# Router on transposed residual rows, modulation at the gather's evacuation, output projection tile by tile

## The chip, the core and the metric

The kernel runs on one core of a Trainium2 chip. The metric is the device time of one execution in microseconds. A core has TensorE (PE in the profile), VectorE (DVE), ScalarE (ACT), GpSimd (POOL) and SyncE (SP), each working through its own queue in order; they hand work to each other by semaphores. DMA queues fill SBUF from HBM.

## What is computed

One decoder layer over 512 tokens of width 1024. The change touches the end of sub-layer 1 and the head of sub-layer 2. Cut to that:

```python
x = x + gate1 * (merged @ w_out[l])
h2 = rmsnorm(x, norm2_g[l]) * (1.0 + scale2) + shift2
# grouped_moe(h2, ...): shared router, 16 experts in 4 groups
logits = t @ router_w + router_b
probs = softmax(logits)
g = argmax over groups of the sum of the top-2 probs
vals, local = top_k(probs of group g, 2)      # weights = vals / sum(vals)
hidden = silu(t @ w_gate) * (t @ w_up)        # per chosen expert
y = sum over experts of weight * (hidden @ w_down)
x = x + gate2 * y
```

`shift2`, `scale2` and the gates are rows of 1024 numbers worked out earlier in the kernel from the condition vector and kept in HBM (`mod_d`).

## The kernel before

Tokens stand in 4 tiles of 128 (`NT`), the width in 8 slices of 128 (`KD`). Every large product is done in three passes (`three`, L612 to L614): both factors are split into a high part in the chip's rounded fp32 (fp32r) and a low rest. A weight chunk of 1 MB is loaded by SP, its high part is written by ACT (`high`, L1087, and `high_e`, L1361) and its low part by DVE (`low`, L1445, and `low_e`, L1759). A chunk then costs PE 48 wide (512-column) multiplies if its 4 products go to 4 banks, or 12 if they go to one.

The output projection `w_out` is done in two halves of 512 columns, `wo0` and `wo1`, two chunks each. `seg` runs chunk by chunk and, in each, over the four token tiles, so that tile m of a half is done only in the last quarter part m of its second chunk. DVE then adds each tile to the residual (`residual`, L1725 and L1727).

After `wo1` comes the router stage. For each token tile: ACT squares and sums the row (`mean_square`, L1318) and takes the root (L1320); DVE inverts it, scales the row (`norm2`, L1734) and adds the shift (L1736), giving fp32 rows `h2f`; ACT and DVE split them into `h2_hi` and `h2_lo` (L1328, L1754); PE turns them (`turn_rows`, L929), ACT copies the turned rows (L1334) and PE multiplies with the router weights (`router`, L936). ACT then has three `high_e` of expert 0 in its queue before the four exponentials (L1368). DVE divides by the sums, ranks (L1778 to L1800), does two `low_e`, and PE counts each expert's tokens in 14 multiplies (L953 to L956). From the counts DVE makes each token's place and the selection matrices (`sel`, L1836).

The experts go in pairs. `gather` (L971) multiplies the split rows with `sel`, 64 multiplies of 256 columns for a pair, in four units of 16; each unit is evacuated by ACT (`hg_high`, L1374) and DVE (`hg_low`, L1862) into `hgT_hi` and `hgT_lo`. Units 2 and 3 reuse the banks of 0 and 1 and wait for their evacuation (`hg_sp`). An expert has 4 up chunks (12 multiplies each) and 2 down chunks. In a pair's second stage PE runs: 4 up chunks, gather units 0 and 1 for the next pair, the down chunks of the expert before, units 2 and 3, the turning of `hid` (L1020). The next stage's up chunk 1 waits for all four units (`hg_sp`, `2 * X + 4`). Six raw buffers and four split buffers carry the chunks; a load waits for `low_e` of the chunk six before it. No planner sets an order: each engine's queue is as written.

## Time and profile before

| | us |
|---|---|
| median of 3 runs | 869.4 |
| lowest and highest | 868.77 and 871.4 |
| the profiled execution | 867.77 |
| its span, first to last instruction | 866.0 |
| PE busy in it | 807.1 (93%) |
| DVE busy | 615.7 (71%) |
| ACT busy | 439.6 (51%) |

The span is divided on the page into 40 slices of 21.65 us; in the row of the granted clock a 9 stands for full speed (2.4 GHz) and a 5 for half (1.2 GHz). Times in the rows are from the span's start. A record of PE carries its pipeline's length, so its start-to-start distance is what an instruction costs in a row of equal ones.

### The profile page before, as it was taken

The numbers are of one execution on the slowest core, as the hardware profiler recorded it, in microseconds if no ns is written. First come the engines' busy times: TensorE is split into PE (matmuls) and PEld (weight loads), VectorE is DVE, ScalarE is ACT, GpSimd is POOL, SyncE is SP. The second block draws the span as 40 slices with busy tenths as digits, with TensorE's granted clock in tenths as the row PEclk, the third lists the DMA queues.
The fourth block names the chain that finished last, engine by engine and source line by source line (L and its number), as shares of the span: only waits on it lengthen the run. The fifth ranks groups of instructions, "written<-read, shape, count | busy, mean of one in ns | idle before, by whom it ended". The sixth has DMA issues, their size and how long they took to land.

```text
span 866.0 us, 10677 instructions
## 1 busy us (share of the span) xinstructions
PE 807.1 (93%) x4014; PEld 643.5 (74%) x4014; DVE 615.7 (71%) x786; ACT 439.6 (51%) x519; POOL 73.4 (8%) x67
## 2 busy tenths in 40 slices
PE   3799999999999889999997779999999999999993
PEld 3687687776666556678886777888888888888882
DVE  4676877425998875536655557888888888888882
ACT  6334224465556345563214607575756566665660
POOL 4020000000000000000000000021111111111111
PEclk9799999999999999999999559999999999999997
DMA  8919993111031112051463245899989898989863
GB/s 257 356 33 386 372 363 141 52 47 50 1 98 49 53 49 74 24 213 63 158 249 132 75 152 179 307 313 318 322 313 337 303 337 310 336 305 334 314 230 51
DMA packets 84330, 174.43 MB, mean 201 GB/s; under 512 B 7696, under 2 KB 27256, under 8 KB 82240
## 3 DMA queue, kind: packets, MB, share of 16 engines
q1 hardware_dynamic: 79200, 156.29, 50.7%
q0 software_dynamic: 5088, 17.59, 8.3%
q8 instruction: 25, 0.41, 0.2%
q14 instruction: 17, 0.14, 0.0%
HBM read 163.34 MB, written 10.52 MB: 201 GB/s over the span
## 4 chain that ended last, share of the span: by engine, by line
PE 81%; DVE 8%; ACT 4%; DMA 3%; issue 2%; SPq 1%; POOL 0%; POOLq 0%; DVEq 0%; ACTq 0%
PE ps L612 19%; PE ps L613 18%; PE ps L614 18%; PE ps L971 7%; PE ps L768 4%; DMA raw<-in_w_in 2%; PE ps L750 1%; DVE w_lo L1445 1%; PE ps L852 1%; PE ps L868 1%; PE ps L880 1%; DMA raw<-in_w_ada 1%; DVE accm L1504 1%; PE ps L783 1%; ACT w_hi L1087 1%
## 5 line engine op out<-in xcount | busy, mean ns | idle before, releaser
L1759 DVE TENSOR_TENSOR w_lo<-raw,w_hi 128x2048 fp32r<-128x2048 f32 x96 | 217.1, 2289 | 22.5 <-ACT w_hi L1361 21.9
L1361 ACT ACTIVATE w_hi<-raw 128x2048 fp32r<-128x2048 f32 x96 | 181.8, 1914 | 15.9 <-PE ps L614 15.9
L612 PE MATMUL ps<-act_lo,w_hi 128*128 128x512 f32 x232 | 98.2, 423 | 7.4 <-DVE act_lo L1487 3.2
L612 PE MATMUL ps<-w_lo,hgT_hi 128*128 128x512 f32 x256 | 101.1, 395 | 0.0
L613 PE MATMUL ps<-w_hi,hgT_lo 128*128 128x512 f32 x256 | 99.7, 390 | 0.0
L614 PE MATMUL ps<-w_hi,hgT_hi 128*128 128x512 f32 x256 | 99.7, 389 | 0.0
L1087 ACT ACTIVATE w_hi<-raw 128x2048 fp32r<-128x2048 f32 (+2 forms) x29 | 52.0, 1794 | 79.7 <-DMA raw<-in_w_in 46.1
L614 PE MATMUL ps<-act_hi,w_hi 128*128 128x512 f32 x232 | 91.1, 393 | 0.0
L613 PE MATMUL ps<-act_hi,w_lo 128*128 128x512 f32 x232 | 90.9, 392 | 0.0
L1445 DVE TENSOR_TENSOR w_lo<-raw,w_hi 128x2048 fp32r<-128x2048 f32 (+2 forms) x29 | 62.0, 2145 | 40.2 <-ACT w_hi L1087 40.1
L591 POOL DMA_INDIRECT out<-ys,slot_tok x16 | 49.3, 3082 | 320.0 <-DVE ys L1855 320.0
L612 PEld LDWEIGHTS ps<-act_lo,w_hi 128*128 128x128 f32 x232 | 43.7, 188 | 32.5 <-issue 16.0
L971 PE MATMUL ps<-sel,act_hi 128*128 128x256 f32 x256 | 64.6, 291 | 3.5 <-DVE sel L1836 3.5
L971 PE MATMUL ps<-sel,act_lo 128*128 128x256 f32 x256 | 64.5, 290 | 0.0
L1374 ACT ACTIVATE hgT_hi<-ps 128x512 fp32r<-128x512 f32 x32 | 19.1, 598 | 79.2 <-PE ps L971 79.2
L614 PEld LDWEIGHTS ps<-w_hi,hgT_hi 128*128 128x128 f32 x256 | 48.1, 188 | 10.2
L612 PEld LDWEIGHTS ps<-w_lo,hgT_hi 128*128 128x128 f32 x256 | 48.1, 188 | 9.6
L613 PEld LDWEIGHTS ps<-w_hi,hgT_lo 128*128 128x128 f32 x256 | 48.1, 188 | 9.4
L971 PEld LDWEIGHTS ps<-sel,act_hi 128*128 128x128 f32 x256 | 51.0, 199 | 4.1 <-issue 3.5
L612 PE MATMUL ps<-w_lo,act_hi 128*128 128x512 f32 x128 | 51.8, 405 | 1.3 <-DVE w_lo L1445 1.3
L612 PE MATMUL ps<-w_lo,hidT_hi 128*128 128x512 f32 x128 | 50.0, 390 | 2.9 <-issue 2.9
L971 PEld LDWEIGHTS ps<-sel,act_lo 128*128 128x128 f32 x256 | 51.0, 199 | 0.5
(260 smaller groups left out, 1497.3 us busy)
## 6 DMA issues: line engine op xcount, KB each, us to landing
raw<-in_w_gate SPq DMA_DIRECT2D x32, 1024.0 KB, 8.5
raw<-in_w_up SPq DMA_DIRECT2D x32, 1024.0 KB, 6.4
raw<-in_w_down SPq DMA_DIRECT2D x32, 1024.0 KB, 8.5
raw<-in_w_in SPq DMA_DIRECT2D x16, 1024.0 KB, 6.7
raw<-in_w_ada SPq DMA_DIRECT2D x16, 1024.0 KB, 7.5
raw<-in_w_ada SPq DMA_DIRECT2D x8, 512.0 KB, 7.0
raw_early<-in_w_ada SPq DMA_DIRECT2D x8, 512.0 KB, 6.2
raw<-in_w_out SPq DMA_DIRECT2D x4, 1024.0 KB, 4.9
```

Of the source, the lines that this page charges most:

```text
L591: pool.indirect_dma_start(out[0], bass.IndirectOffsetOnAxis(slot_tok[:, X % 2:X % 2 + 1], 0), ys[X % 2][:, :], None, compute_op=ALU.add).t ...
L612: pe.matmul(o, a[0], b[1], start=start, stop=False)
L613: pe.matmul(o, a[1], b[0], start=False, stop=False)
L614: return pe.matmul(o, a[0], b[0], start=False, stop=stop)
L750: last = pe.matmul(zt[m % 2][:, r, 0:S - P * i], head(kaT, 2 * hp + r, P * i, P * i + P), head(qaT, 2 * hp + r, P * i, S), start=True, sto ...
L768: pe.matmul(zt[m % 2][:, r, P * (j - i):S - P * i], lhs[:, :], sp_tile(hp, j)[:, r, :], start=False, stop=False, skip_group_check=True)
L971: last = pe.matmul(ps[2 + u % 2][:, 2 * P * (kk % 2):2 * P * (kk % 2) + 2 * P], part[:, tt, P * kk:P * kk + P], sel[:, tt, :, :], start=(t ...
L1087: act.activation(cols(w_hi[spl_slot[w]], 0, top, nk), cols(raw[raw_slot[n]], 0, top, nk), ACT.Copy).then_inc(hi_ready, 1)
L1361: act.activation(e_hi[s_][:, :], e_raw[r][:, :], ACT.Copy).then_inc(e_top, 1)
L1374: act.activation(hgT_hi[:, :, 2 * u:2 * u + 2, :].rearrange("p b k s -> p k b s"), ps[2 + u % 2][:, :].rearrange("p (k b s) -> p k b s", k ...
L1445: dve.tensor_tensor(lo, r, hi.bitcast(F32), ALU.subtract).then_inc(chunk_split, 1)
L1759: dve.tensor_tensor(e_lo[s_][:, :], e_raw[r][:, :], e_hi[s_][:, :].bitcast(F32), ALU.subtract).then_inc(e_split, 1)
```

## The change

- **Router.** It no longer takes modulated rows. PE turns the residual rows themselves (`xres`, raw) and multiplies them with `rwm`, the router weights times (1 + scale2) * norm2_g; DVE then scales the 16 logits of a token with the row's reciprocal deviation (`rstd`) and adds `lbias`, the product of the shift with the router weights plus the router's bias (`logit_bias`, 8 multiplies of 16 columns on PE). Softmax's denominators go, since the ranks and the weights' ratio don't need them.
- **Rows for the gather.** `h2_hi` and `h2_lo` are the residual rows times the reciprocal deviation only, straight from `xres` (`rows_high`, `rows_low`). Scale and shift come in at the evacuation of the gather: `hg_high` is now two instructions of 256 columns with a scale and a bias column, followed by two that take the shift off again (`hm`); `hg_low` two of 256 columns.
- **`wo1`** is done tile by tile (`out_cols`: tile m over the first chunk, then over the second), with the turning and the routers between. It has split buffers 2 and 0, where `wo0` and `wo1` had 0 and 1 in turn.
- **Order.** `low_e(0)` stands ahead of the second half's residual, `low_e(1)` and `low_e(2)` behind the first gather's evacuation; their `high_e` behind the exponentials. Squares are taken by half rows. The count is 5 multiplies instead of 14 (the first of 64 columns, then 64, 48, 32 and 16). Expert chunks 4 and 5 are loaded after `wo1`, into the space of the merged activations.
- **Small loads.** The three broadcast rows of 512 KB become three columns of 1024 single elements, issued once the attention has ended; `gate2` waits for the routers.

Cut to its core; functions of before that go are printed above, and their removal isn't repeated:

```diff
-    e_raw = [raw[2], raw[3], at("raw4", [CH], F32, 136), raw[0], raw[1], at("raw5", [CH], F32, 186)]
-    e_hi = [w_hi[2], w_hi[0], w_hi[1], at("w_hi3", [CH], F32R, 112)]
-    e_lo = [w_lo[2], w_lo[0], w_lo[1], at("w_lo3", [CH], F32R, 120)]
+    e_raw = [raw[2], raw[3], raw[0], raw[1], at("raw4", [CH], F32, 80), at("raw5", [CH], F32, 88)]
+    e_hi = [w_hi[1], w_hi[2], w_hi[0], at("w_hi3", [CH], F32R, 112)]
+    e_lo = [w_lo[1], w_lo[2], w_lo[0], at("w_lo3", [CH], F32R, 120)]
...
-        spl_slot = [(w + 2) % SPL if w < W_PROJ else (w - W_PROJ) % 2 for w in range(N_W)]
+        spl_slot = [(w + 2) % SPL if w < W_PROJ else (w - W_PROJ) % 2 if w < N_W - 2 else (2, 0)[w - N_W + 2] for w in range(N_W)]
...
-                        elif z == 2:
-                            sp.wait_ge(seg_ready, seg_done("oa1", 3))
-                        elif z < 5:
-                            sp.wait_ge(chunk_split, N_RAW - 5 + z + 1)
+                        elif z < 4:
+                            sp.wait_ge(chunk_split, N_RAW - 3 + z)
                         else:
-                            sp.wait_ge(r_ps, NT)
+                            sp.wait_ge(seg_ready, seg_done("wo1", 3))
...
-            pool.wait_ge(seg_ready, seg_done("ob1", 3))
-            for dst, src in ((shift2, mod_d[0][:, D:2 * D]), (amp2, mod_d[1][:, 0:D]), (g2row, norm2_g)):
-                pool.dma_start(dst[:, :], src.partition_broadcast(P).rearrange("p a d -> p (a d)")).then_inc(ld_r2, 16)
+            pool.wait_ge(ob_ps, 2 * NT)
+            for dst, src in ((sc2c, mod_d[1][0, 0:D]), (sh2c, mod_d[0][0, D:2 * D]), (g2c, norm2_g[0])):
+                pool.dma_start(dst[:, :], src.rearrange("(k p) -> p k", p=P), allow_slow_non_contiguous=True
+                               ).then_inc(ld_r2, 16)
...
-            pool.wait_ge(h2_sp, NT)
-            pool.wait_ge(h2T_ps, 2 * NT)
+            pool.wait_ge(r_ps, NT)
...
+            def turn_x1(half, tt):
+                n = n_turned[0]
+                n_turned[0] += 1
+                pe.wait_ge(x1_ready, 4 * half + tt + 1)
+                if n >= 3:
+                    pe.wait_ge(x1T_act, n - 2)
+                for k in range(4):
+                    a = 512 * half + P * k
+                    last = pe.transpose(ps[n % 3][:, P * k:P * k + P], xres[:, tt, a:a + P], ident[:, :])
+                last.then_inc(x1T_ps, 1)
...
+            def router(tt, k0=0, k1=KD):
+                o = ps[4][:, 0:N_EXP] if tt == 3 else ps[3][:, N_EXP * tt:N_EXP * tt + N_EXP]
+                if tt < 3:
+                    pe.wait_ge(x1T_act, 5 + tt)
+                    pe.wait_ge(lb_ok, 1)
+                    pe.wait_ge(r_lg, tt) if tt else None
+                elif k0 == 0:
+                    pe.wait_ge(x1T_act, 4)
+                    pe.wait_ge(x1_ready, 5)
+                else:
+                    pe.wait_ge(x1T_dve, 1)
+                for k in range(k0, k1):
+                    lhs = x1T_a[:, tt, k, :] if k < 4 else x1T_b[tt % 2][:, k - 4, :]
+                    last = pe.matmul(o, lhs, rwm[:, k, :], start=(k == 0), stop=(k == KD - 1))
+                if k1 == KD:
+                    last.then_inc(r_ps, 1)
...
+            out_cols(0, 0, 0, 4)
+            turn_x1(0, 0)
+            turn_x1(0, 1)
+            out_cols(0, 1, 0, 4)
+            turn_x1(0, 2)
+            turn_x1(0, 3)
+            logit_bias()
+            out_cols(1, 0, 0, 4)
+            turn_x1(1, 0)
+            out_cols(1, 1, 0, 4)
+            router(0)
+            out_cols(2, 0, 0, 4)
+            turn_x1(1, 1)
+            out_cols(2, 1, 0, 4)
+            router(1)
+            out_cols(3, 0, 0, 4)
+            turn_x1(1, 2)
+            out_cols(3, 1, 0, 2)
+            router(2)
+            out_cols(3, 1, 2, 4)
+            router(3, 0, 4)
+            turn_x1(1, 3)
+            router(3, 4, KD)
...
+            def x1_copy(half, tt):
+                n = 4 * half + tt
+                act.wait_ge(x1T_ps, n + 1)
+                if half and tt >= 2:
+                    act.wait_ge(r_ps, tt - 1)
+                dst = x1T_b[tt % 2][:, :, :] if half else x1T_a[:, tt, :, :]
+                act.activation(dst, ps[n % 3][:, :].rearrange("p (k s) -> p k s", k=4), ACT.Copy).then_inc(x1T_act, 1)
             def rows_high(tt):
+                act.wait_ge(h2_rs, tt + 1)
+                act.activation(h2_hi[:, tt, :], xres[:, tt, :], ACT.Copy, scale=st[:, tt, 5:6]).then_inc(h2_hiR, 1)
...
+                square(0, tt)
+            act.preload_act_table_set("sqrt_and_others")
+            high_e(0, 0, 1)
+            for tt in range(NT):
+                x1_copy(0, tt)
+            for tt in range(NT - 1):
+                square(1, tt)
+                deviation(tt)
+                x1_copy(1, tt)
+                rows_high(tt)
+            square(1, NT - 1)
+            deviation(NT - 1)
+            act.preload_act_table_set("natural_log_exp_and_others")
+            for tt in range(NT):
+                act.wait_ge(r_lg, tt + 1)
+                act.activation(comb[:, tt, :], comb[:, tt, :], ACT.Exp, bias=nmax[:, tt:tt + 1]).then_inc(r_exp, 1)
+            rows_high(NT - 1)
+            high_e(1, 1, 1)
+            high_e(2, 2, 1)
 
             def hg_high(X, u):
                 act.wait_ge(hg_ps, 2 * X + u + 1)
+                for j in range(2):
+                    kk = 2 * u + j
+                    last = act.activation(hgT_hi[:, :, kk, :], ps[2 + u % 2][:, 2 * P * j:2 * P * j + 2 * P].rearrange(
+                        "p (b s) -> p b s", b=2), ACT.Identity, bias=sh2c[:, kk:kk + 1], scale=amp2c[:, kk:kk + 1])
+                last.then_inc(hg_hi, 1)
+                act.wait_ge(hg_hi, 2 * X + u + 1)
+                for j in range(2):
+                    kk = 2 * u + j
+                    last = act.activation(hm[u % 2][:, j, :, :], hgT_hi[:, :, kk, :].bitcast(F32), ACT.Identity,
+                                          bias=nsh2c[:, kk:kk + 1])
+                last.then_inc(hg_hm, 1)
...
+            def prepare():
+                dve.wait_ge(ld_r2, 48)
+                link(dve.scalar_tensor_tensor(out=amp2c[:, :], in0=sc2c[:, :], scalar=1.0, in1=g2c[:, :], op0=ALU.add,
+                                              op1=ALU.mult))
+                dve.tensor_tensor(rwm[:, :, :], rw[:, :, :], amp2c[:, :].unsqueeze(2).broadcast_to([P, KD, N_EXP]), ALU.mult)
+                dve.tensor_scalar(nsh2c[:, :], sh2c[:, :], -1.0, None, ALU.mult)
+                dve.tensor_copy(shb[:, :, :], sh2c[:, :].unsqueeze(2).broadcast_to([P, KD, P])).then_inc(prep_ok, 1)
+            def rstd(tt):
                 dve.wait_ge(h2_sd, tt + 1)
+                dve.reciprocal(st[:, tt, 5:6], st[:, tt, 5:6]).then_inc(h2_rs, 1)
+            def rows_low(tt):
+                dve.wait_ge(h2_hiR, tt + 1)
+                dve.scalar_tensor_tensor(out=h2_lo[:, tt, :], in0=xres[:, tt, :], scalar=st[:, tt, 5:6],
+                                         in1=h2_hi[:, tt, :].bitcast(F32), op0=ALU.mult, op1=ALU.subtract).then_inc(h2_sp, 1)
+            def logit(tt):
+                dve.wait_ge(r_ps, tt + 1)
+                dve.wait_ge(h2_rs, tt + 1)
+                src = ps[4][:, 0:N_EXP] if tt == 3 else ps[3][:, N_EXP * tt:N_EXP * tt + N_EXP]
+                link(dve.scalar_tensor_tensor(out=comb[:, tt, :], in0=src, scalar=st[:, tt, 5:6], in1=lbias[:, :],
+                                              op0=ALU.mult, op1=ALU.add))
+                dve.tensor_reduce(nmax[:, tt:tt + 1], comb[:, tt, :], AX.X, ALU.max, negate=True).then_inc(r_lg, 1)
...
             raw_chunks(2)
+            prepare()
             dve.wait_ge(ld_x2, 16)
             dve.wait_ge(ld_g1, 16)
+            residual(0, 0)
+            raw_chunks(1)
+            for m in range(1, 4):
                 residual(0, m)
+            dve.wait_ge(h2_ss, NT)
+            dve.tensor_scalar(st[:, :, 4:5], st[:, :, 2:3], 1.0 / D, EPS, ALU.mult, ALU.add).then_inc(h2_base, 1)
...
+            dve.wait_ge(lb_ps, 1)
+            dve.tensor_tensor(lbias[:, :], ps[3][:, 64:64 + N_EXP], rb[:, :], ALU.add).then_inc(lb_ok, 1)
+            dve.wait_ge(lb_ok, 1)
             low_e(0, 0)
+            residual(1, 0)
+            rstd(0)
+            residual(1, 1)
+            rows_low(0)
+            logit(0)
+            rstd(1)
+            residual(1, 2)
+            rows_low(1)
+            logit(1)
+            rstd(2)
+            rows_low(2)
+            residual(1, 3)
+            logit(2)
+            dve.wait_ge(x1T_ps, 2 * NT)
+            dve.wait_ge(r_ps, 2)
+            dve.tensor_copy(x1T_b[1][:, :, :], ps[1][:, :].rearrange("p (k s) -> p k s", k=4)).then_inc(x1T_dve, 1)
+            rstd(3)
+            logit(3)
             dve.wait_ge(r_exp, NT)
...
-            for cc in (1, 2):
-                low_e(cc, cc)
+            rows_low(3)
...
-                dve.wait_ge(hg_hi, 2 * X + u + 1)
-                part = lambda t: t[:, :, 2 * u:2 * u + 2, :].rearrange("p b k s -> p k b s")
-                dve.tensor_tensor(part(hgT_lo), ps[2 + u % 2][:, :].rearrange("p (k b s) -> p k b s", k=2, b=2),
-                                  part(hgT_hi).bitcast(F32), ALU.subtract).then_inc(hg_sp, 1)
+                dve.wait_ge(hg_hm, 2 * X + u + 1)
+                for j in range(2):
+                    kk = 2 * u + j
+                    last = dve.scalar_tensor_tensor(
+                        out=hgT_lo[:, :, kk, :], in0=ps[2 + u % 2][:, 2 * P * j:2 * P * j + 2 * P].rearrange(
+                            "p (b s) -> p b s", b=2), scalar=amp2c[:, kk:kk + 1], in1=hm[u % 2][:, j, :, :], op0=ALU.mult,
+                        op1=ALU.subtract)
+                last.then_inc(hg_sp, 1)
...
+                    low_e(1, 1)
+                    low_e(2, 2)
```

PE at the end of the router stage, before: rows of tile 3 are turned, two routers follow, then the 14 multiplies that count (only the first of them stands here).

```order
L929 MATMUL ps<-ident,h2f_120 128x128 x3
L929 MATMUL ps<-ident,h2f_120 128x128 [waits h2T_sb]
L929 MATMUL ps<-ident,h2f_120 128x128 x3
L936 MATMUL ps<-rw,h2T 128x16 [waits h2T_sb]
L936 MATMUL ps<-rw,h2T 128x16 x7
L936 MATMUL ps<-rw,h2T 128x16 [waits h2T_sb]
L936 MATMUL ps<-rw,h2T 128x16 x7
L954 MATMUL ps<-comb,before 128x16 [waits route_sel]
```

After: of the last tile only its second half is left to turn when `wo1` has ended, and the count is five multiplies.

```order
L956 MATMUL ps<-rwm,x1T_a 128x16 [waits x1_ready,x1T_by_act]
L956 MATMUL ps<-rwm,x1T_a 128x16 x3
L933 MATMUL ps<-ident,xres 128x128 [waits x1T_by_act,x1_ready]
L933 MATMUL ps<-ident,xres 128x128 x3
L956 MATMUL ps<-rwm,x1T_b_120 128x16 [waits x1T_by_dve]
L956 MATMUL ps<-rwm,x1T_b_120 128x16 x3
L1001 MATMUL ps<-comb,before 128x64 [waits route_sel]
L1004 MATMUL ps<-comb,ones 128x64
L1004 MATMUL ps<-comb,ones 128x48
L1004 MATMUL ps<-comb,ones 128x32
```

What moved: three of the four routers and seven of the eight turnings stand among the wide multiplies of `wo1`, ahead of this place.

DVE between the two halves of the output projection, before (`w_lo` here is the second chunk of `wo1`, and `etmp` the residual's product with the gate):

```order
L1725 TENSOR_TENSOR etmp_114<-ps,gate_115 128x512 [waits seg_ready]
L1727 TENSOR_TENSOR xres<-xres,etmp_114 128x512 [waits evac_low]
L1445 TENSOR_TENSOR w_lo_59<-raw_50,w_hi_56 128x2048 [waits hi_ready]
L1745 SCALAR_TENSOR_TENSOR amp_122<-amp_122,g2row 128x1024 [waits ld_rows2]
L1725 TENSOR_TENSOR etmp_113<-ps,gate_115 128x512 [waits seg_ready,dve_chain]
L1727 TENSOR_TENSOR xres<-xres,etmp_113 128x512 [waits evac_high]
L1725 TENSOR_TENSOR etmp_114<-ps,gate_115 128x512 [waits seg_ready]
```

After, from the last residual of the first half to the first of the second:

```order
L1789 TENSOR_TENSOR xres<-xres,etmp_115 128x512 [waits evac_low]
L1787 TENSOR_TENSOR etmp_116<-ps,gate_117 128x512 [waits seg_ready]
L1789 TENSOR_TENSOR xres<-xres,etmp_116 128x512 [waits evac_low]
L1826 TENSOR_SCALAR st<-st 128x4 [waits h2_ss]
L1834 TENSOR_TENSOR lbias<-ps,rb 128x16 [waits logit_bias_ps]
L1830 TENSOR_TENSOR w_lo_59<-raw_51,w_hi_56 128x2048 [waits expert_hi,logit_bias]
L1787 TENSOR_TENSOR etmp_115<-ps,gate_117 128x512 [waits seg_ready]
L1789 TENSOR_TENSOR xres<-xres,etmp_115 128x512 [waits evac_high]
```

What moved: `low_e(0)` (L1830, `w_lo` from `raw`) stands behind a wait for PE's `logit_bias` and ahead of the residual that PE's next turning needs.

DVE from the selection matrices to the first expert's fourth chunk, before:

```order
L1836 TENSOR_TENSOR sel<-iota,posm 128x4x128 x2
L1862 TENSOR_TENSOR hgT_lo<-ps,hgT_hi 128x2x2x128 [waits hg_hi] x4
L1824 CAST slot_t<-tid 128x64
L1825 CAST slot_t<-comb 128x64
L1826 TENSOR_TENSOR slot_t<-comb,slot_t 128x64 [waits dve_chain]
L1759 TENSOR_TENSOR w_lo_148<-raw_49,w_hi_147 128x2048 [waits expert_hi,ld_gate2]
```

After, from the evacuation of gather unit 2:

```order
L1946 SCALAR_TENSOR_TENSOR hgT_lo<-ps,amp2c,hm_145 128x2x128 [waits hg_less_shift]
L1946 SCALAR_TENSOR_TENSOR hgT_lo<-ps,amp2c,hm_145 128x2x128
L1946 SCALAR_TENSOR_TENSOR hgT_lo<-ps,amp2c,hm_146 128x2x128 [waits hg_less_shift]
L1946 SCALAR_TENSOR_TENSOR hgT_lo<-ps,amp2c,hm_146 128x2x128
L1830 TENSOR_TENSOR w_lo_60<-raw_52,w_hi_57 128x2048 [waits expert_hi]
L1830 TENSOR_TENSOR w_lo_58<-raw_49,w_hi_55 128x2048 [waits expert_hi]
L1907 CAST slot_t<-tid 128x64
L1908 CAST slot_t<-comb 128x64
L1909 TENSOR_TENSOR slot_t<-comb,slot_t 128x64 [waits dve_chain]
L1830 TENSOR_TENSOR w_lo_155<-raw_50,w_hi_154 128x2048 [waits expert_hi,ld_gate2]
```

What moved: `low_e(1)` and `low_e(2)`, which stood ahead of the count, stand behind the last unit, and a unit is two instructions.

## Rows read from the trace of the kernel before

**Rows 1.** The page: the granted clock in 40 slices
```profile
PEclk9799999999999999999999559999999999999997
```

**Rows 2.** Windows: us, busy time (and instructions) by engine, granted clock, DMA share, GB/s
```profile
490.00:520.00 30.00, 20.19 (x109) 20.01 (x110) 16.23 (x42) 7.36 (x14) 0.00 (x0) 0.57 0.42 144
...
560.00:600.00 40.00, 40.00 (x217) 34.64 (x216) 34.19 (x26) 24.75 (x19) 6.22 (x2) 1.00 0.93 315
```

**Rows 3.** Chain of work, 448 to 532 us: start, us, what
```profile
485.19 1.80 PE ps L929 x8
...
487.51 5.50 ACT w_hi L1361 x3
493.03 1.28 ACT L1368
...
499.69 0.23 DVE comb L1797
...
509.58 10.60 PE ps L971 x64
...
530.86 0.24 PE ps L614
```

**Rows 4.** Timeline of PE, 467 to 512 us: start, us, instruction, idle time before
```profile
469.42 0.39 PE L614 MATMUL ps<-w_hi,act_hi 128*128 128x512 f32 x1
...
481.76 3.43 PE L936 MATMUL ps<-rw,h2T 128*128 128x16 f32 x16
...
499.97 0.61 PE L954 MATMUL ps<-comb,before 128*128 128x16 f32 x2 [6.35 <-DVE comb L1797]
...
509.58 0.55 PE L971 MATMUL ps<-sel,act_hi 128*128 128x256 f32 x1 [3.46 <-DVE sel L1836]
```

**Rows 5.** Timeline of DVE, same stretch: same columns
```profile
461.76 0.69 DVE L1725 TENSOR_TENSOR etmp<-ps,gate 128x512 f32<-128x512 f32 x1 [8.23 <-PE ps L614]
...
496.10 0.42 DVE L1778 TENSOR_TENSOR r_gt<-comb 128x256 f32<-128x256 f32 x1
...
506.16 0.17 DVE L1805 COPY counts<-ps 128x16 f32<-128x16 f32 x1 [1.11 <-PE ps L956]
```

**Rows 6.** Groups by shape on ACT, then DVE: count, busy, mean ns of one, idle before
```profile
L1374 ACT ACTIVATE hgT_hi<-ps 128x512 fp32r<-128x512 f32 x32 | 19.1, 598 | 79.2 <-PE ps L971 79.2
...
L1256 ACT ACTIVATE lrow<-lrow,nmax 128x256 f32<-128x256 f32 x8 | 4.0, 500 | 4.9 <-DVE nmax L1653 4.9
...
L1275 ACT ACTIVATE obT_hi<-ps 128x256 fp32r<-128x256 f32 x8 | 3.0, 370 | 1.3 <-PE ps L880 1.3
...
L1112 ACT ACTIVATE hfull<-ps,mod 128x512 f32<-128x512 f32 x1 | 0.8, 777 | 2.7 <-DVE mod L1481 2.7
...
L1759 DVE TENSOR_TENSOR w_lo<-raw,w_hi 128x2048 fp32r<-128x2048 f32 x96 | 217.1, 2289 | 22.5 <-ACT w_hi L1361 21.9
...
L1862 DVE TENSOR_TENSOR hgT_lo<-ps,hgT_hi 128x512 fp32r<-128x512 f32 x32 | 21.5, 689 | 25.2 <-ACT hgT_hi L1374 25.2
...
L1592 DVE SCALAR_TENSOR_TENSOR score<-relu_tmp,wi,score 128x256 f32<-128x256 f32 x7 | 3.4, 483 | 0.1
```

**Rows 7.** Timelines of ACT, DVE and PE round one hand-over between expert pairs
```profile
599.75 0.60 ACT L1374 ACTIVATE hgT_hi<-ps 128x512 fp32r<-128x512 f32 x1 [1.32 <-PE ps L971]
...
600.39 0.69 DVE L1862 TENSOR_TENSOR hgT_lo<-ps,hgT_hi 128x512 fp32r<-128x512 f32 x1 [1.23 <-ACT hgT_hi L1374]
...
603.11 4.49 DVE L1759 TENSOR_TENSOR w_lo<-raw,w_hi 128x2048 fp32r<-128x2048 f32 x2
...
602.75 0.39 PE L612 MATMUL ps<-w_lo,hgT_hi 128*128 128x512 f32 x1
```

**Rows 8.** Windows across the fall and the rise of the clock, columns as Rows 2
```profile
474.00:475.00 1.00, 0.00 (x0) 0.00 (x0) 0.96 (x3) 0.91 (x1) 0.53 (x1) 0.88 0.00 0
...
515.50:516.00 0.50, 0.50 (x5) 0.50 (x5) 0.00 (x0) 0.00 (x0) 0.00 (x0) 0.79 0.00 0
```

**Rows 9.** The column load into c_col (1024 single elements): issue to landing
```profile
DMA to landing us min/median/max: 2.2/2.2/2.2
```

186 lines of the change are left out of this document (68 added, 118 removed).

## The prediction, made blind

> **What bounds the kernel now.** I read the page's clock row first: it stands at 9 nearly throughout and falls to 5 in one place, slices 26 and 27 [rows 1]. There the windows show PE busy for 20.19 of 30 us at a clock of 0.57, while in the expert loop it is busy 40.00 of 40 us at full clock, with DVE at 34.64, ACT at 24.75 and a DMA share of 0.93 [rows 2]. So the loop is PE's, and what can be won lies where the clock is low. The chain there is a walk between engines: turnings (485.19), then three weight splits on ACT (487.51, 5.50 us) and a table load (1.28) ahead of the exponentials, DVE's ranking until 499.69 plus 0.23, PE's count, and the first gather at 509.58, itself at half clock for most of its 10.60 us; the first expert's up chunks end at 530.86 + 0.24 = 531.1 [rows 3]. The last wide multiply of `wo1` is issued at 469.42 and one costs 0.227, so `wo1` ends at 469.65 [rows 4]. From there to the gather it is 509.58 - 469.65 = 39.9 us. That is the stretch that the change attacks, and it pays for it before and behind.
>
> **Part 1, `wo1` with work between (a cost).** `wo1` is 96 wide multiplies of 0.227, so it began at 469.65 - 21.8 = 447.9. Put between them now: 7 turnings of four transposes, the shift's product and three routers of 8 multiplies. Before, eight transposes took 1.80 us at half clock [rows 3], 0.225 each; 16 router records (two to a multiply) took 3.43, 0.214 each [rows 4]. `wo1` runs at full clock, so I take half of both: 28 x 0.112 = 3.1 and 64 x 0.107 = 6.8, together 9.9 us. If the narrow records did not gain from the clock it would be 6.3 + 13.7 = 20.0; below 9.9 no reason points.
> There is one more wait. `logit_bias` ends at about 456.9 (12 + 12 wide multiplies, four turnings, itself), and DVE waits for it ahead of `low_e(0)`, 2.29 us [rows 6]. Then the residual of tile 0 takes two instructions of 0.69 [rows 5], so it is ready at 457.3 + 2.3 + 1.4 = 461.0. PE has finished tile 1's first chunk at 459.6 and stands before the turning of tile 0: 1.5 us. Behind it tile by tile DVE's residual (1.4) fits beside 2.7 us of wide multiplies, and ACT's copies too, so I see no second wait. `wo1` now ends at 469.65 + 9.9 + 1.5 = 481.1, which is 11.4 later.
>
> **Part 2, from the last wide multiply to the gather (the gain).** Last tile: residual ready 1.7 us on (482.8), four transposes (0.5), DVE's copy of a 512-column bank (0.69 as for the same width in [rows 6]), the last four router multiplies (8 records, 0.9), all with 0.1 a hand-over: 485.2. ACT squares half a row, takes the root and loads the exponential's table (1.28) meanwhile, until 485.3. Two small DVE instructions for the logits (0.4) and the last exponential (0.3) bring 486.3. From there DVE's ranking is as before less the normalisation: from 496.10 [rows 5] to 499.92 [rows 3], 3.8, so 490.1. The three splits of 5.50 us are gone from this path, and so is any wait for a raw chunk. The count is 10 records for 28: before, from 499.97 [rows 4] to 506.16 [rows 5], 6.2; now 10 x 0.214 = 2.1 plus a pipeline of 0.3, 492.5. `rows_low` of tile 3 (1.3) fits beside it. Then the places and `sel`, 509.58 - 506.16 = 3.4, as before: the gather starts at about 495.9. The stretch is 14.8 us for 39.9, a gain of 25.1. Bounds: four or five hand-overs that I put too short add up to 3; a path in which the exponentials of tiles 0 to 2 are done early takes 1 off.
>
> **Part 3, the gather's evacuation and the first expert (a cost).** The rows show no instruction with scale and bias columns and 256 columns. A plain copy of 512 columns takes 0.598; with both columns (L1112) 0.777, so 0.18 more. A plain copy of 256 takes 0.370, one with a bias column 0.500 [rows 6]. So a unit on ACT is 2 x 0.55 + 2 x 0.50 less an overlap of 0.1 at two places, 1.9 us, for 0.60; on DVE two of 0.483 less 0.1, 0.9, for 0.69. Ends: 1.5 (four plain ones) and 2.5 (no overlap and slow hand-overs).
> The Trainium skill states the same surcharge (ScalarE: Activation LUTs, What ACT_TABLE_LOAD costs): about 93 ns for each column operand, and as much overlap between neighbours. By it a unit would be 2 x 0.585 + 2 x 0.49 - 0.28 = 1.9. The rule speaks against this change, and the rows agree with it.
> In the first gather unit 3 waits for unit 1's evacuation, 2.9 us against one unit's 1.92 of multiplies (16 x 0.12) and its own start-up: 1.2 us of wait. Up chunk 1 then waits for unit 3's evacuation and, behind it, `low_e(1)`: 2.9 + 2.3 = 5.2 against 2.7 of chunk 0, 2.5 us. `low_e(2)` and `low_e(3)` keep up with PE. Together 3.7 us. Both splits had been done before the gather; the cover is gone. The loads are no issue: chunks 4 and 5 start at 481 and are wanted at 510 or later.
>
> **Part 4, the loop.** At each of 7 hand-overs the last unit's ACT copy starts at 599.75, DVE ends at 600.39 + 0.69 = 601.08, and PE wants it at 602.75: slack 1.67 [rows 7]. Added are 1.3 on ACT and 0.2 on DVE, 1.5 us. The slack just holds; I allow 0.1 each, 0.8 in all. The delay is handed on in DVE's queue to the weight split for up chunk 3, which PE starts two chunks later, at 602.75 + 2 x 2.72 = 608.2; the first of the two splits from 603.11 on ended half way, at 605.4 [rows 7], so 1.5 fits. In a pair of 42 us DVE and ACT have idle time to catch up [rows 2]. So nothing accumulates. Ends: 0 and 7 x 1.0.
> The three column loads: in another place such a load of 1024 single elements landed in 2.2 us [rows 9], and here they have over 40 us. I cost them at nothing.
> Of them the Trainium skill says (DMA: Bandwidth & Descriptors, Rules for kernel authors) that a non-contiguous last dimension becomes one descriptor per element and should be avoided; by that rule the change would look bad, but the row shows a small price, and three of them would be well hidden.
>
> **The sum.** -25.1 + 11.4 + 3.7 + 0.8 = -9.2 us. Against the profiled execution that is 867.77 - 9.2 = 858.6; that execution lies 1.6 under the median of the three runs, by which it would be 860.2. I take 859.4 between them.
>
> **The clock.** After the last wide multiply the clock held about 5 us, with a few transposes in them, and fell in the window at 474; it rose in the one at 515.5, 6 us into the gather, although PE had run narrow records from 481.76 to past 487 without a gap [rows 3, 4, 8]. So narrow work does not keep it up. I assume the same two marks: it falls in the tail and the gather's first 6 us run at half.
>
> **Rivals.**
> 1. Smaller gain: `wo1` is stretched more. Narrow records at 0.15 instead of 0.107, or a wait of 1 us before each later turning. For it: each turning waits for a residual that DVE makes behind other work in the same queue. Against: 2.7 us of wide multiplies cover 1.4. Price 3 to 6 us: 863 to 866.
> 2. Slower: the hand-over becomes the loop's bound. ACT's eight added instructions and DVE's two-step units exceed the slack of 1.67 by more than they do in my working. It decides from 1.4 us of loss a hand-over: 7 x 1.4 = 9.8 eats the gain of 10.0 that the sum has without its 0.8, and with 1.5 to 2 us each the time is 869 to 873. For it: the DMA share of 0.93 and DVE's 34.64 of 40 leave little room to catch up [rows 2]. Against: ACT has 15 us idle in 40.
> 3. Larger gain: the tail is 2 us shorter, or the clock rises earlier or never falls (the gather then takes 7.7 for 10.6 us). 853 to 856.
> 4. No change: what is put into `wo1` is as long as what it saves, because the low clock reaches into it. Against: in the attention stage PE mixes narrow and wide work and the row of the clock shows 9 [rows 1]. If it happened, 10 us of wide work at half clock would cost 10 more: 868 to 870.
>
> **Chances.** Forecast (855 to 863) 0.60; rival 1 0.14; rival 2 0.07; rival 3 0.13; rival 4 0.06. A measurement of this kernel can tell 0.3%, 2.6 us, from no change. Below 866.8 lie the forecast, rivals 1 and 3: 0.87. Rival 4 is half within, so same 0.05 and slower 0.08. For 8 in 10 I take the forecast, most of rival 3 and most of rival 1: 853 to 866.
>
> **What would show it.** Right: last wide multiply of `wo1` at 481 with a wait of 1.5 us before the fifth turning; gather at 496; its unit 3 waiting 1.2 us; 2.5 us of wait at expert 0's chunk 1; ACT's evacuation instructions at 0.55 and 0.50; a pair of experts still at 42 us. Wrong: waits of PE on `hg_split` in every pair, a clock of 0.5 inside `wo1`, or a gather start later than 500.

## The result, and the profile after

The changed kernel takes 860.9 us (median of 4 runs, 860.69 to 861.29) beside 870.4 us for the kernel before on the same chip (868.77 to 872.84, 4 runs). The ratio is 0.989, with a 95% interval of 0.986 to 0.992: faster by 1.1%. The forecast was 859.4. On a second chip the changed kernel was measured again (run `c1_changed`, below): 0.989 once more, 0.986 to 0.993.

The profiled execution of the changed kernel has a time of 861.29 us and a span of 859.6, against 867.77 and 866.0 before. So the two traces explain 6.4 us of span; the medians are 9.5 apart. I come back to these 3 us at the end of the point by point part.

The clock row of the page has lost its trough; where [rows 1] show two slices at 5, it now reads:

```profile
PEclk9799999999999999999999889999999999999997
```

TensorE's timeline from `wo1` to the first expert's turning, which answers to [rows 4] (start, us, instruction, idle time before it and what ended it). L933 turns a tile of residual rows, L956 is the router, L1001 and L1004 count, L1021 is the gather:

```profile
450.70 1.03 PE L933 MATMUL ps<-ident,xres 128*128 128x128 f32 x8
...
460.99 0.66 PE L933 MATMUL ps<-ident,xres 128*128 128x128 f32 x4 [1.05 <-DVE xres L1789]
464.24 0.96 PE L956 MATMUL ps<-rwm,x1T_a 128*128 128x16 f32 x8
...
481.60 0.96 PE L956 MATMUL ps<-rwm,x1T_a 128*128 128x16 f32 x8
483.27 0.66 PE L933 MATMUL ps<-ident,xres 128*128 128x128 f32 x4 [0.71 <-DVE xres L1789]
484.71 1.07 PE L956 MATMUL ps<-rwm,x1T_b 128*128 128x16 f32 x8 [0.78 <-DVE x1T_b L1852]
490.50 0.69 PE L1001 MATMUL ps<-comb,before 128*128 128x64 f32 x2 [4.72 <-DVE comb L1881]
490.99 1.83 PE L1004 MATMUL ps<-comb,ones 128*128 128x64 f32 x8
496.28 0.55 PE L1021 MATMUL ps<-sel,h_hi 128*128 128x256 f32 x1 [3.46 <-DVE sel L1919]
502.96 0.38 PE L1021 MATMUL ps<-sel,h_hi 128*128 128x256 f32 x1 [1.05 <-DVE hgT_lo L1946]
512.30 0.47 PE L615 MATMUL ps<-w_lo,hgT_hi 128*128 128x512 f32 x1 [2.51 <-DVE w_lo L1830]
523.16 0.66 PE L1070 MATMUL ps<-ident,hid 128*128 128x128 f32 x4 [0.85 <-DVE hid L1969]
```

The router of the last tile starts at 481.60, right behind the last wide multiply, and the gather at 496.28. Before, that stretch went from 469.65 to 509.58 [rows 3, 4].

The clock in the same stretch (windows; the last four columns are POOL's busy time, the granted clock, the DMA share and GB/s):

```profile
486.00:487.00 1.00, 0.00 (x0) 0.00 (x0) 0.59 (x4) 1.00 (x4) 0.54 (x1) 0.59 0.88 258
496.30:499.00 2.70, 2.70 (x13) 2.70 (x14) 0.00 (x0) 0.00 (x0) 0.00 (x0) 0.50 0.03 6
499.00:500.00 1.00, 1.00 (x7) 1.00 (x7) 0.00 (x0) 0.00 (x0) 0.00 (x0) 0.59 0.00 0
...
514.00:516.00 2.00, 2.00 (x6) 1.63 (x5) 1.97 (x5) 0.00 (x0) 0.00 (x0) 0.50 0.96 338
...
840.00:845.00 5.00, 4.81 (x14) 3.84 (x15) 0.09 (x1) 0.00 (x0) 1.54 (x1) 0.66 0.56 79
```

It falls near 486.2, 4.6 us after the last wide multiply, and is back at 499.8, 3.5 us into the gather. (In a window of one microsecond a clock of 0.59 means that it stood at half for four fifths of it.) Then come two more falls that I had not forecast: at half clock (0.50 in 514 to 516) eight multiplies of the first expert run, soon behind chunk 1's wait of 2.51 us, and again eight of the last down chunks behind the last turning. Both waits stand in TensorE's timeline, the second here:

```profile
836.68 0.60 PE L1070 MATMUL ps<-ident,hid 128*128 128x128 f32 x4
840.19 0.47 PE L615 MATMUL ps<-w_lo,hidT_hi 128*128 128x512 f32 x1 [2.91 <-issue]
...
847.13 0.39 PE L617 MATMUL ps<-w_hi,hidT_hi 128*128 128x512 f32 x1
```

The evacuation of the gather on ScalarE and VectorE, unit 0 of the first gather:

```profile
500.04 1.02 ACT L1429 ACTIVATE hgT_hi<-ps,sh2c,amp2c 128x256 fp32r<-128x256 f32 x2 [8.80 <-PE ps L1021]
501.09 0.91 ACT L1435 ACTIVATE hm<-hgT_hi,nsh2c 128x256 f32<-128x256 f32 x2
502.03 0.88 DVE L1946 SCALAR_TENSOR_TENSOR hgT_lo<-ps,amp2c,hm 128x256 fp32r<-128x256 f32 x2 [5.90 <-ACT hm L1435]
```

And the loop, 40 us of it, to be held against the second window of [rows 2]:

```profile
575.00:615.00 40.00, 40.00 (x216) 34.49 (x215) 34.35 (x34) 29.72 (x31) 4.46 (x3) 1.00 0.93 319
```

The waits of the stretch 550 to 830 us hold one on the evacuation (PEld's; us in total, times, longest):

```profile
PEld ps L615 <- DVE hgT_lo L1946: 1.4, 7, 0.2
```

TensorE is still busy for the whole 40 us. ScalarE has gone up from about 25 to 30. The three column loads, issued from 382.9 on, landed 2.9, 2.9 and 3.3 us later and are first used at 434.8, so they cost nothing, as forecast (op, KB, us from issue to landing):

```profile
sc2c<-mod_scratch POOLq DMA_DIRECT2D x1, 4.0 KB, 2.9
sh2c<-mod_scratch POOLq DMA_DIRECT2D x1, 4.0 KB, 2.9
g2c<-in_norm_g POOLq DMA_DIRECT2D x1, 4.0 KB, 3.3
```

**How the experiments are read.** Single runs of one kernel differ by up to 9 us, and in the profiles most of this arises in the first 100 us. The first turning of `wo1` comes at 450.70 in the profile above, at 454.21 in that of the same kernel on the second chip and at 457.57 in a variant that is identical up to there (e1); of these 6.9 us between first and last, 5.7 stand already at the first product of `acc` with `ones` (99.53 and 105.24). So beside each ratio I cut the profile into stretches by TensorE's own marks: T, the first turning (first L933); G, the gather's first multiply; H, the first turning of `hid`; L, the last turning of `hid`; M, the last multiply. Each number is a difference of two starts in the timeline. For the kernel before, G to H is 531.94 - 509.58. T to G is left blank where the turnings stand behind `wo1`, since T is then another place.

| kernel | T to G | G to H | H to L | L to M | median, us | ratio to before (95%) |
|---|---|---|---|---|---|---|
| before | | 22.36 | 312.98 | 8.84 | 870.4 | |
| changed | 45.58 | 26.88 | 313.52 | 10.45 | 860.9 | 0.989 (0.986 to 0.992) |
| changed, second chip (c1) | 45.50 | 26.86 | 313.43 | 10.44 | 860.9 | 0.989 (0.986 to 0.993) |
| e1_low0 | 44.64 | 26.28 | 313.46 | 10.42 | 858.8 | 0.986 (0.984 to 0.989) |
| e2_low12 | 45.57 | 23.61 | 313.49 | 8.84 | 858.1 | 0.985 (0.982 to 0.988) |
| e3_undo | | 26.91 | 313.44 | 10.45 | 869.5 | 0.999 (0.997 to 1.001) |
| e4_fill | 45.01 | 25.35 | 313.41 | 8.82 | 858.0 | 0.985 (0.982 to 0.987) |
| e5_best | 43.21 | 20.20 | 313.55 | 8.84 | 850.8 | 0.979 (0.976 to 0.982) |
| e6_hm2 | 45.51 | 28.04 | 326.17 | 10.46 | 876.2 | 1.008 (1.005 to 1.010) |
| e7_exps | 49.01 | 26.46 | 313.53 | 10.44 | 864.3 | 0.994 (0.992 to 0.996) |
| e8_fill_two | 45.77 | 26.38 | 313.39 | 8.84 | 861.1 | 0.990 (0.986 to 0.993) |
| e9_before_exps | | 21.49 | 312.98 | 10.44 | 869.2 | 0.999 (0.997 to 1.002) |
| e10_no_fill | 43.79 | 22.26 | 313.49 | 10.43 | 856.7 | 0.985 (0.982 to 0.988) |
| e11_no_shift | 45.57 | 23.62 | 312.95 | 11.71 | 859.7 | 0.989 (0.986 to 0.993) |

The two profiles of the changed kernel agree to 0.1 us in every stretch. Between variants the clock's falls and rises come at other times, and G to H can move by a microsecond through that alone. Each stretch is from one profiled execution, so differences below 1 us in it are read with that in mind. The medians of the kernel before, against which the ratios of the three later comparisons stand, are 871.3 (e1 to e4), 870.9 (c1, e5 to e7) and 869.8 us (e8 to e11).

### The profile page after: what moved, and what is told of

Same layout as the page of the kernel before. It is cut to its first block, busy times and chain, and to the rows that moved or that the text cites. A ratio compares the mean times of both kernels' runs of the same rounds, so it can differ in the third digit from the quotient of the medians.

```text
span 859.6 us, 10823 instructions
## 1 busy us (share of the span) xinstructions
PE 801.4 (93%) x4010; PEld 633.8 (74%) x4012; DVE 612.0 (71%) x820; ACT 479.9 (56%) x618; POOL 74.3 (9%) x67
## 4 chain that ended last, share of the span: by engine, by line
PE 82%; DVE 7%; ACT 4%; DMA 3%; issue 2%; SPq 1%; POOL 0%; POOLq 0%; DVEq 0%; ACTq 0%
PE ps L615 20%; PE ps L617 19%; PE ps L616 19%; PE ps L1021 7%; PE ps L771 4%; DMA raw<-in_w_in 1%; PE ps L753 1%; PE ps L855 1%; DVE w_lo L1507 1%; PE ps L871 1%; PE ps L883 1%; DMA raw<-in_w_ada 1%; DVE accm L1566 1%; PE ps L786 1%; ACT w_hi L1137 1%
## 5 line engine op out<-in xcount | busy, mean ns | idle before, releaser
L1830 DVE TENSOR_TENSOR w_lo<-raw,w_hi 128x2048 fp32r<-128x2048 f32 x96 | 215.6, 2286 | 16.8 <-ACT w_hi L1402 16.8
L1402 ACT ACTIVATE w_hi<-raw 128x2048 fp32r<-128x2048 f32 x96 | 180.0, 1909 | 11.3 <-PE ps L617 11.3
L1021 PE MATMUL ps<-sel,h_hi 128*128 128x256 f32 x256 | 63.6, 288 | 4.5 <-DVE sel L1919 3.5
L1021 PE MATMUL ps<-sel,h_lo 128*128 128x256 f32 x256 | 63.4, 287 | 0.0
L617 PEld LDWEIGHTS ps<-w_hi,hgT_hi 128*128 128x128 f32 x256 | 48.4, 189 | 10.4
L1429 ACT ACTIVATE hgT_hi<-ps,sh2c,amp2c 128x256 fp32r<-128x256 f32 x64 | 32.7, 562 | 41.7 <-PE ps L1021 41.7
L1021 PEld LDWEIGHTS ps<-sel,h_hi 128*128 128x128 f32 x256 | 50.1, 196 | 5.3 <-issue 3.5
L617 PEld LDWEIGHTS ps<-act_hi,w_hi 128*128 128x128 f32 x232 | 44.0, 190 | 10.0
```

Of the source, the lines that this page charges most:

```text
L617: return pe.matmul(o, a[0], b[0], start=False, stop=stop)
L1021: last = pe.matmul(ps[2 + u % 2][:, 2 * P * (kk % 2):2 * P * (kk % 2) + 2 * P], part[:, tt, P * kk:P * kk + P], sel[:, tt, :, :], start=(t ...
L1402: act.activation(e_hi[s_][:, :], e_raw[r][:, :], ACT.Copy).then_inc(e_top, 1)
L1429: last = act.activation(hgT_hi[:, :, kk, :], ps[2 + u % 2][:, 2 * P * j:2 * P * j + 2 * P].rearrange("p (b s) -> p b s", b=2), ACT.Identit ...
L1830: dve.tensor_tensor(e_lo[s_][:, :], e_raw[r][:, :], e_hi[s_][:, :].bitcast(F32), ALU.subtract).then_inc(e_split, 1)
```

## Experiments

### What of the tail belongs to which order

The prediction gave the stretch from the last wide multiply to the gather one price, 25.1 us. Three kernels take it partly apart. **e3_undo** keeps all of the change but puts TensorE's order in `wo1` back:

```diff
             out_cols(0, 0, 0, 4)
-            turn_x1(0, 0)
-            turn_x1(0, 1)
             out_cols(0, 1, 0, 4)
-            turn_x1(0, 2)
-            turn_x1(0, 3)
             logit_bias()
             out_cols(1, 0, 0, 4)
...
+            out_cols(3, 1, 0, 4)
+            turn_x1(0, 0)
...
+            turn_x1(0, 3)
+            turn_x1(1, 0)
+            router(0)
+            turn_x1(1, 1)
+            router(1)
+            turn_x1(1, 2)
+            router(2)
             router(3, 0, 4)
```

> The changed kernel with the order on TensorE alone undone: the wide multiplies of wo1 stand together (tile by tile, the router's bias after the first tile), the turnings and the routers of tiles 0 to 2 behind them. Moved out of wo1 are 28 turnings (3.1 us), 48 records of routers (5.1 us) and the wait of 1.05 us, so the wide multiplies should end about 9.3 us earlier, near 472.3. Theory A (TensorE keeps its full clock through turnings and routers since it has few gaps, and ScalarE's chain of square, root, copy and rows, 2.8 us for each tile, sets the pace): the router of tile 3 ends about where it did, gather at about 497, time 860 to 862. Theory B (the clock falls some 5 us after the last wide multiply, as the prediction took for its tail, and turnings and routers run at half clock, 4.3 us a tile): gather at about 502, time 865 to 867. Theory C (the order of wo1 is what the whole gain rests on): all of the 25.1 us of the tail comes back against 9.3 us saved, time above 870.

Measured: ratio 0.999, which can't be told from 1, so by the time the gain of the change is gone. TensorE's timeline and three windows:

```profile
475.60 1.06 PE L956 MATMUL ps<-rwm,x1T_a 128*128 128x16 f32 x8 [1.67 <-ACT x1T_b L1383]
...
479.58 1.89 PE L956 MATMUL ps<-rwm,x1T_a 128*128 128x16 f32 x8 [0.69 <-ACT x1T_b L1383]
481.31 1.87 PE L956 MATMUL ps<-rwm,x1T_b 128*128 128x16 f32 x8
...
504.20 0.55 PE L1020 MATMUL ps<-sel,h_hi 128*128 128x256 f32 x1 [3.46 <-DVE sel L1918]
```

```profile
475.00:477.00 2.00, 1.40 (x13) 1.40 (x13) 1.83 (x4) 1.98 (x4) 0.14 (x1) 1.00 1.02 350
477.00:479.00 2.00, 1.89 (x9) 1.49 (x9) 1.87 (x5) 0.69 (x4) 0.41 (x1) 0.50 0.99 353
479.00:494.00 15.00, 12.65 (x56) 11.74 (x56) 6.52 (x14) 7.10 (x14) 1.07 (x3) 0.50 0.48 183
```

The turnings start at 471.43 (forecast 472.3), the clock falls at 477 and stays down, although TensorE is busy for 12.65 of the 15 us from 479 on, and eight router records take 1.87 to 1.89 us where they take 0.96 inside `wo1`. `wo1` began at 447.8 as in the changed kernel's trace (its shift product starts at 453.26, 24 wide multiplies or 5.44 us in), so the gather at 504.20 is 8 us later than the 496.28 of the changed kernel. That is theory B, with the gather 2 us later than its 502; the waits on ScalarE's copies (1.67 us, and 0.69 twice) stand on the path and are enough for that. The time of 869.5 is above theory B's 865 to 867 and nearly theory C's: of the 13.3 us by which the gather comes earlier in the changed kernel 5.4 are still there, and the costs behind it (G to H 26.91, L to M 10.45) use them up. Theory A, that the narrow work itself keeps the clock up, is out.

**e7_exps** undoes one thing on ScalarE, in the changed kernel:

```diff
             deviation(NT - 1)
+            high_e(1, 1, 1)
+            high_e(2, 2, 1)
             act.preload_act_table_set("natural_log_exp_and_others")
```

(the two lines are gone from behind `rows_high(NT - 1)`)

> The changed kernel with one part undone: high_e(1) and high_e(2), 3.7 us on ScalarE, stand ahead of the exponentials again, behind the root of tile 3. Theory A (the exponentials' start sets the tail, as the prediction had it): the exponentials end 3.7 us later, the gather starts 3.7 us later, time about 864.5. Rival B (the logits of tile 3 come late anyhow and hide part): in the changed kernel the logit ends 0.1 us after the table load, so less than 0.5 us can be hidden; a rise under 2 us would need another cover. Rival C (a longer wait of TensorE ahead of the counts moves the fall and rise of its clock too): 1 to 2 us on either side of 864.5.

```profile
482.80 3.69 ACT L1402 ACTIVATE w_hi<-raw 128x2048 fp32r<-128x2048 f32 x2
486.50 1.28 ACT L1419 ACT_TABLE_LOAD   x1
487.80 0.90 ACT L1422 ACTIVATE comb<-comb,nmax 128x16 f32<-128x16 f32 x4
```

T to G grows from 45.5 to 49.0 us: 3.4 of the 3.7 come through, and the ratio moves from 0.989 to 0.994. Theory A holds.

**e9_before_exps** makes the same edit alone, in the kernel before:

```diff
-            for cc in range(3):
-                high_e(cc, cc, 1)
+            high_e(0, 0, 1)
             for tt in range(NT):
                 act.wait_ge(r_lg, 1)
                 act.activation(comb[:, tt, :], comb[:, tt, :], ACT.Exp, ...)
+            high_e(1, 1, 1)
+            high_e(2, 2, 1)
```

> The kernel before the change, with one part of the change alone: high_e(1) and high_e(2), 3.7 us on ScalarE, stand behind the exponentials instead of ahead of them. Theory A (in the order of the kernel before the splits were hidden behind the routers, whose last result reaches VectorE at 493.66 and whose maximum is ready at 494.1, while the splits and the table load end at 494.3): the exponentials start 0.2 us earlier, the gather with them, time 0.2 us less than before. Rival B (the prediction's sentence that three splits of 5.50 us leave the path): 3.7 us less. It tells how much of the 25.1 us of the tail is owed to the order on ScalarE and how much to the routers' place.

```profile
473.99 1.03 PE L929 MATMUL ps<-ident,h2f 128*128 128x128 f32 x8
...
513.77 0.55 PE L971 MATMUL ps<-sel,act_hi 128*128 128x256 f32 x1 [3.46 <-DVE sel L1837]
```

From the first turning to the gather it is 39.78 us, against 509.58 - 469.65 = 39.93 in the kernel before: 0.15 us. The ratio is 0.999 and can't be told from 1. So the same edit is worth 0.15 us in the old order and 3.4 in the new one. Before, the splits lay beside the routers; once the routers are hidden in `wo1`, the splits are what would be left.

From the start of `wo1` to the gather it is therefore 61.7 us before, 61.6 with ScalarE's order alone, 56.4 with all but TensorE's order, 48.3 with everything. TensorE's order is worth 8 us with the rest in place; what it would be worth alone no run shows. Of the 5.3 us between 61.7 and 56.4 the shorter count is 3.8: from its first multiply to VectorE's copy of the counts it is 506.16 - 499.97 = 6.2 us before and 492.86 - 490.50 = 2.4 in the changed kernel. The other 1.5 (ScalarE's splits, the denominators, the shorter chain ahead of the router) are not taken apart. VectorE's copy in the changed kernel:

```profile
492.86 0.17 DVE L1888 COPY counts<-ps 128x16 f32<-128x16 f32 x1 [0.49 <-PE ps L1004]
```

### The two waits that the change adds ahead of the experts

**e1_low0** moves `low_e(0)` on VectorE:

```diff
             dve.wait_ge(lb_ok, 1)
-            low_e(0, 0)
             residual(1, 0)
...
             rstd(1)
+            low_e(0, 0)
             residual(1, 2)
```

> The changed kernel with one VectorE instruction moved: low_e(0) (2.29 us, issued at 457.31 between the router's bias and residual(1,0)) stands behind rstd(1). In the changed kernel's trace TensorE waits 1.05 us at 460.99 for the first turned tile of the second half. Theory A (the queue of VectorE makes that wait, as the prediction said): the wait goes, the wide multiplies of wo1 end 1.0 us earlier (about 480.5 instead of 481.5), and the time falls by 0.7 to 1.1 us, to about 860.0. Rival B (the wait is only passed on to the next turning or to the routers, which are close behind): wo1 ends within 0.2 us of where it ended, time unchanged.

```profile
466.65 0.60 PE L933 MATMUL ps<-ident,xres 128*128 128x128 f32 x4
...
519.19 0.47 PE L615 MATMUL ps<-w_lo,hgT_hi 128*128 128x512 f32 x1 [2.51 <-DVE w_lo L1830]
```

The wait of 1.05 us is gone from the fifth turning and T to G is 0.9 us shorter, as theory A had it. The two ratios' intervals overlap, so the time alone would not show it. The profile shows one thing more: here chunk 1 stands behind the very same wait of 2.51 us, and no half clock follows (9.30 us from there to H, 10.86 in the changed kernel). G to H is only 0.6 us shorter for it, since the clock rose 5.8 us into the gather instead of 3.5 and chunk 0 starts 1.0 us later after G.

**e2_low12** takes away the other wait:

```diff
                         low_e(EC * X0 + cc, cc)
+                else:
+                    low_e(1, 1)
+                    low_e(2, 2)
                 for u in range(4):
                     hg_low(X0, u)
                 if isinstance(X0, int):
-                    low_e(1, 1)
-                    low_e(2, 2)
                     slot_rows()
```

> The changed kernel with two VectorE instructions moved: low_e(1) and low_e(2) (4.5 us together) stand ahead of the first evacuation of the gather, where VectorE is idle for 5.9 us (496.13 to 502.03), instead of behind the fourth. In the changed kernel's trace TensorE waits 2.51 us for low_e(1) at 512.30, and from there to about 516.7 its wide multiplies run at half clock (granted clock 0.50 between 514 and 516). Theory A (the half clock follows from the wait): both go; chunk 1 starts about 2.5 us earlier and some 4.4 us of multiplies at half clock become 2.2: the first stage ends 4.7 us earlier, time about 856.3. Rival B (the clock falls there by something else, the wait alone goes): 2.5 us, time about 858.4. Rival C (the weights' arrival or high_e(3) on ScalarE is next and takes the gain back in chunk 3): under 1 us, time about 860.

```profile
516.13 0.50 PE L615 MATMUL ps<-w_lo,hgT_hi 128*128 128x512 f32 x1 [0.22 <-DVE hgT_lo L1946]
525.43 0.66 PE L1070 MATMUL ps<-ident,hid 128*128 128x128 f32 x4 [0.85 <-DVE hid L1969]
```

G to H is 23.6 instead of 26.9, 3.3 us less: the wait and the half clock behind it are both gone. That the one brought the other, as theory A says, is not shown by this, since e1 kept the wait and had no half clock either. It is less than the 4.7 of theory A for two reasons that the stretches show: a late rise of the clock in this profile's gather (4.9 us in instead of 3.5), and a half clock that cost 1.6 us, not 2.2. Rival C is out: nothing in chunk 3 takes the gain back.

### What the evacuation costs

**e11_no_shift** takes part of the evacuation away: it leaves the shift of the second modulation out of the computation, and with it the step `hm`, so it is not a kernel to use. **e6_hm2** does the step `hm` twice. In e11's diff VectorE's side is cut: `hg_low` waits for `hg_hi` and subtracts `hgT_hi`.

```diff
-                        "p (b s) -> p b s", b=2), ACT.Identity, bias=sh2c[:, kk:kk + 1], scale=amp2c[:, kk:kk + 1])
+                        "p (b s) -> p b s", b=2), ACT.Copy, scale=amp2c[:, kk:kk + 1])
...
-                act.wait_ge(hg_hi, 2 * X + u + 1)
-                for j in range(2):
-                    last = act.activation(hm[u % 2][:, j, :, :], ...)
```

> The changed kernel without the shift in the gather's evacuation (left out of the computation: the shift of the second modulation; ScalarE only multiplies by the scale, and the step hm, which takes the shift off again, is gone). A unit costs ScalarE 1.0 us instead of 1.93. Theory A (the evacuation's length is paid for in the first gather and not in the loop): unit 2 waits 0.1 us instead of 1.05, low_e(1) starts behind the fourth unit about 2 us earlier, from the gather to the first turning 24.9 us for 26.9, a pair of experts 42.2 us as ever, its waits of 0.2 us gone: time 858.5. Rival B (the loop's hand-overs pay, too): a pair comes down from 42.25 us to 42.0 or less, 2 us over the loop, time 856 to 857.

```profile
512.24 0.47 PE L615 MATMUL ps<-w_lo,hgT_hi 128*128 128x512 f32 x1 [1.39 <-DVE w_lo L1824]
521.50 0.66 PE L1070 MATMUL ps<-ident,hid 128*128 128x128 f32 x4 [0.85 <-DVE hid L1963]
```

Unit 2's wait is gone and chunk 1's is 1.39 us instead of 2.51; G to H is 3.3 us shorter, of which 1.6 is the half clock that did not come this time and 1.7 the evacuation's (a little more, as the clock rose 1.4 us later here than in the changed kernel). H to L is 312.95, to 0.03 us what it was before the change, and 0.5 to 0.6 less than in the changed kernel. So both theories have a part: the loop does pay, but 0.5 us in all. The ratio, 0.989, does not tell it apart from the changed kernel.

```diff
                 act.wait_ge(hg_hi, 2 * X + u + 1)
+                for j in range(2):
+                    kk = 2 * u + j
+                    last = act.activation(hm[u % 2][:, j, :, :], hgT_hi[:, :, kk, :].bitcast(F32), ACT.Identity,
+                                          bias=nsh2c[:, kk:kk + 1])
+                last.then_inc(hx, 1)
+                act.wait_ge(hx, 2 * X + u + 1)
                 for j in range(2):
```

> The changed kernel with the step that takes the shift off again (hm) done twice on ScalarE in every unit, 0.91 us more a unit and a small wait between. Theory A (the slack at the hand-over is used up, as the prediction had it: 1.67 us of slack against 1.5 added, and the profile shows waits of 0.2 us): each of the 7 hand-overs in the loop now waits for two units in a row, 1.8 to 2.0 us each, 13 us, and the first gather about 3 us: time 875 to 878, a pair of experts 44.1 us for 42.25. Rival B (ScalarE is busy only 30 of 40 us in the loop and its idle time takes the step up): a pair stays at 42.3 us, only the first gather pays, time 863 to 865.

Its waits between 550 and 845 us, and one of them in the timeline:

```profile
PE ps L616 <- DVE hgT_lo L1953: 11.1, 7, 1.6
```

```profile
597.94 0.50 PE L616 MATMUL ps<-w_lo,hgT_hi 128*128 128x512 f32 x1 [1.58 <-DVE hgT_lo L1953]
```

Seven waits of 1.58 us, and H to L is 12.7 us longer, 1.81 for each hand-over, which is two units of 0.91. There is no slack left. ScalarE's idle quarter does not help, since the step stands in a chain that TensorE waits for. The time, 876.2, is theory A's. (The first stage pays only 1.2 us and not 3: its waits grow by 2.5, but chunk 1, now behind a wait of 3.45 us, had no half clock.) This is rival 2 of the prediction made real: the change is one evacuation step away from it.

### The clock

**c1_changed** is the changed kernel itself, with no edit, beside other variants.

> The changed kernel itself once more, beside the other variants on one chip, to see which marks of its profile come back. Theory A (the half clock behind the wait for low_e(1), 512.30 to about 516.7, and behind the last turning, 841.2 to 844.6, are bound to the work that stands before them): both come back. Rival B (they depend on when the clock is next set and not on the kernel's work alone): one or both are missing, 1.6 us each. Median by the ratio of the first comparison, 0.989, about 861.

```profile
516.00:520.00 4.00, 4.00 (x13) 3.09 (x12) 3.97 (x5) 0.00 (x0) 0.00 (x0) 0.60 0.74 258
```

Both falls came back, here behind chunk 1's wait (0.60), and behind the last turning (L to M 10.44), although everything happened 3.5 us later in the span. So they looked bound to the work; but e1 and e7, with the same wait at chunk 1 and changes well ahead of it alone, have no fall there, nor has e6 behind 3.45 us. Rival B is nearer: neither the wait nor its length decides alone. What does stays open. In e1 and e7 the clock had risen 5.8 and 6.2 us into the gather, in the three profiles with a half-clock gather and a fall (the two of the changed kernel, e3) 3.4 to 3.5; but e6 had 3.5 and no fall, so this is no rule either.

**e4_fill** puts multiplies of no use into TensorE's waits (**e8_fill_two** does it at two other places, **e5_best** and **e10_no_fill** are a pair with and without):

```diff
+            def filler(n, o, a, r):
+                for i_ in range(n):
+                    pe.matmul(o, a, r, start=True, stop=True)
...
             router(3, 4, KD)
+            filler(14, ps[0][:, :], h2_hi[:, 0, 0:P], h2_hi[:, 0, 0:512])
             pe.wait_ge(r_sel, 1)
...
             last.then_inc(pos_ps, 1)
+            filler(10, ps[0][:, :], h2_hi[:, 0, 0:P], h2_hi[:, 0, 0:512])
...
                 stage(X0 + N_EXP - 1, N_EXP - 1, 1, False, True)
+                filler(9, ps[2][:, :], hgT_hi[:, 1, 0, :], hgT_hi[:, 1, 0:4, :])
```

> The changed kernel with multiplies added that compute nothing used (128x512, into a free bank): 14 behind router(3), where TensorE then waits 4.72 us, 10 behind the counts, where it waits 3.46 us, and 9 behind the last turning, where it waits 2.91 us. At full clock they take 3.2, 2.3 and 2.1 us and fit into the waits. Theory A (the clock falls because TensorE is idle there): it stays at 1.00 up to and through the gather, the counts take 0.95 us instead of 1.83, the first 16 multiplies of the gather 1.9 us instead of 3.73, and the multiplies after the last turning stay at 0.23 us each where eight of them took 0.43: 0.9 + 1.8 + 1.6 = 4.3 us less, time about 856.6. Rival B (the clock falls all the same, by what came before): the fillers at half clock take 6.0 and 4.3 us, longer than the waits: 2 to 3 us more, time 863 to 864. Rival C (what is gained at the gather is lost again at the wait for low_e(1)): 1.6 to 2.5 us less, time 858.5 to 859.3.

```profile
485.77 5.05 PE L962 MATMUL ps<-h_hi 128*128 128x512 f32 x14
490.66 0.43 PE L1006 MATMUL ps<-comb,before 128*128 128x64 f32 x2
490.92 1.02 PE L1009 MATMUL ps<-comb,ones 128*128 128x64 f32 x8
```

```profile
486.00:488.00 2.00, 2.00 (x7) 1.51 (x7) 1.52 (x8) 2.00 (x6) 0.53 (x1) 0.61 0.82 249
...
490.00:492.00 2.00, 2.00 (x15) 1.70 (x14) 1.83 (x7) 1.39 (x1) 0.00 (x0) 1.00 1.03 415
```

No theory fits whole. The clock falls all the same near 486.4, with TensorE already back at wide work since 485.77, so most of the first 14 fillers run at half clock (5.05 us); but it is up again at 490, and counts and gather run at full speed: the counts' ten records take 1.4 us for 2.5, the gather's first units are at 0.12 a multiply. H to L is untouched, and behind the last turning there is no fall (L to M 8.82). The half clock behind chunk 1's wait came in this run too. From T to the end it is 405.2 us against 408.9.

**e8_fill_two** tried the two unforecast falls:

```diff
                 up_chunk(X, 0, b, z0, z)
+                if fresh:
+                    filler(9, ps[1][:, :], hgT_hi[:, 0, 0, :], hgT_hi[:, 0, 0:4, :])
...
+                filler(9, ps[2][:, :], hgT_hi[:, 1, 0, :], hgT_hi[:, 1, 0:4, :])
                 down(X0 + N_EXP - 1, 10, EC * (X0 + N_EXP) - 2)
```

> The changed kernel with 9 multiplies of 128x512 (2.1 us) into a free bank at two places only: behind up chunk 0 of expert 0, inside the wait of 2.51 us for low_e(1), and behind the last turning, inside the wait of 2.91 us. In two profiles of the changed kernel the clock falls behind both waits and the multiplies after them take 1.6 us longer each time. Theory A (TensorE's idleness in the wait brings the fall): no fall at either place, 3.2 us less, time about 857.7. Rival B (the fall comes from what ran earlier, and the fillers then run at half clock, 3.9 us in waits of 2.5 and 2.9): 1 to 3 us more, 862 to 864. Rival C (only one of the two is due to idleness): 859.3. Where the clock would not have fallen anyway, the fillers change nothing.

```profile
839.64 2.33 PE L962 MATMUL ps<-hgT_hi 128*128 128x512 f32 x9
842.79 0.47 PE L615 MATMUL ps<-w_lo,hidT_hi 128*128 128x512 f32 x1 [0.82 <-issue]
```

No fall at either place, and L to M is 8.84. For the last turning the count over all profiles speaks, though it doesn't prove: without fillers there the multiplies behind it are slowed in 9 of 11 (L to M 10.4 to 11.7; the kernel before and e2 are the exceptions at 8.84), with them in 0 of 3. For chunk 1 it does not: without a filler and with the wait of 2.5 us or more, the fall came in 4 of 7 (both profiles of the changed kernel, e3, e4; not e1, e6, e7), so that its absence here proves nothing. Nor did it gain its 1.6 us: as in e1 and e7 the clock rose late, 6.0 us into the gather, and G to H is 0.5 shorter. What is left, 1.6 us behind the last turning and this 0.5, is below what the time can show: the ratio is 0.990, and theory A's 857.7 was not reached (861.1).

### The parts together

**e5_best** has e1, e2 and the fillers of e4. It also gives the first gather's units 2 and 3 banks of their own (4 and 1), so that they don't wait for an evacuation, and moves the normalised weights, the overflow flag and the clearing of the slot table behind `sel`. **e10_no_fill** is the same without fillers.

> All shortenings together: low_e(0) behind rstd(1); low_e(1) and low_e(2) ahead of the first evacuation; the fillers of 14, 10 and 9 wide multiplies; the first gather in four banks, so that its unit 2 doesn't wait for unit 0's evacuation (1.05 us in the changed kernel); and the normalised weights, the overflow flag and the clearing of the slot table behind the selection instead of ahead of it (0.6 us). Theory A (they add up): from the first turning to the gather 43.5 us for 45.6, from the gather to the first turning of hid 20.0 us for 26.9 (four evacuation units in a row, 1.9 + 4 x 1.93 + 0.9, then 9.3 us), from the last turning to the last multiply 8.8 for 10.4: together 10.6 us less than the changed kernel, time 850 to 852. Rival B (the earlier start meets the arrival of chunks 3 to 5 or high_e(3), which on ScalarE stands behind the fourth unit): 3 to 4 us of that are lost in chunk 3 or in the first loads of the loop, time 854 to 856.

> The variant with all shortenings, without its fillers. Theory A (the fillers are worth what the clock costs: 0.8 us at the counts, 1.8 to 3 us in the first gather, 1.6 us behind the last turning): 4.2 to 5.4 us more than with them, 855 to 856.5; from the gather to the first turning of hid about 22 us for 20.2. Rival B (without the idle time that the other edits took out, the clock rises early enough anyway): under 2 us more, 851 to 853.

e5_best takes 850.8 us, ratio 0.979 (0.976 to 0.982), with G to H at 20.20 and T to G at 43.21 (forecast 20.0 and 43.5): theory A, the edits add up. It beats both kernels: 2.1% under the kernel before and, by the two ratios, 1.0% under the changed one. In its profile the clock stays up in the tail, where the first 14 fillers take 3.44 us:

```profile
484.00:488.00 4.00, 3.00 (x14) 2.13 (x12) 3.30 (x17) 4.00 (x6) 0.53 (x1) 1.00 0.95 325
```

The same fillers at the same place did not hold it in e4; what decides between the two stays open. Without the fillers it is 856.7, ratio 0.985: by the stretches 0.6 us more up to the gather, 2.1 from there to H and 1.6 behind the last turning, 4.2 in all, which is theory A's lower end; the two ratios are 0.006 apart, 5.2 us. Against the changed kernel the edits without fillers take 1.8 us out of T to G and 4.6 out of G to H.

## Why the prediction was right, point by point

**Part 1, `wo1`: +11.4, measured +11.8.** From 447.98 (twelve wide multiplies ahead of the first turning) to 481.60 it is 33.6 us for 21.8. A router's 16 records took 1.7 us, 0.106 each (forecast 0.107), a transpose about 0.10 (forecast 0.112). The wait ahead of the fifth turning is there, from the named cause, 1.05 us for 1.5. What the sum left out are the seams: each piece of narrow work put between costs 0.1 to 0.15 us, about 1 in all. By luck they replace what the wait and the transposes lacked.

**Part 2, last wide multiply to gather: 14.8, measured 14.7.** Each mark is within 0.4 us: residual 483.2 for 482.8, exponentials to 486.6 for 486.3, counts handed over at 492.9 for 492.5, gather at 496.28 for 495.9. But the sentence that the three splits are "gone from this path" says less than it seems to: in the old order they cost 0.15 us (e9). They would have become the bound in the new one (e7, 3.4 us). Of the 25.2 us gained here 18.1 are the place of the turnings and routers and the half clock that they ran at (e3, without it, still has 32.8 us from the last wide multiply to the gather), at a price of 10 in `wo1`; 3.8 are the shorter count. The splits' move is a condition of the first.

**Part 3, evacuation and first expert: +3.7, measured +4.5.** ScalarE's instructions took 0.562 and 0.502 us for 0.55 and 0.50, a unit 1.93 for 1.9. The Trainium skill's surcharge for a column operand (ScalarE: Activation LUTs, What ACT_TABLE_LOAD costs) gives 0.585 and 0.49; the trace agrees within 0.03. Chunk 1's wait was forecast at 2.5 and is 2.51. The 1.2 us of unit 3 came as 1.05 us of unit 2: with unit 0 evacuated 1.0 + 0.9 + 0.9 us after its last multiply and unit 1 multiplied in 1.9, it is unit 2 that comes too early. Two errors about the clock lie beside this and partly cancel: I took the gather's first 6 us at half clock, as before, and they were 3.5, about 1.1 us in its favour; and I did not see that the clock can fall again behind a wait of 2.5 us, 1.6 us against it.

**Part 4, the loop: +0.8, measured +0.5.** H to L is 313.5 for 313.0, and seven waits of 0.2 us stand where I allowed 0.1 each. By its letter the sign of being wrong, a wait on `hg_split` in every pair, is there; its size is what the sum allowed. That the slack of 1.67 "just holds" against 1.5 is what e6 shows from the other side: the next 0.91 us a unit come through whole. Rival 2 had 0.07; its mechanism was real, and the change stays just short of it.

**Not in the sum: the last turning.** L to M is 10.45 for 8.84. No part of the change reaches there. The fall behind that wait is also in e9, whose end is the old kernel's. So the profile of the kernel before was probably one of the few without it.

**The sum by the traces** is -13.3 (span's start to gather, 11.8 - 25.2 and 0.1 of a later start of `wo1`), +4.5, +0.5, +1.6 and +0.2 after the last multiply: -6.4 us with the roundings. The medians say -9.5. Of the 3 us between them, 2.6 are that the profiled execution of the kernel before lies that far under its median of 870.4, and the 1.6 of the last turning are likely part of that; where the rest arises stays open. The forecast of -9.2 was thus right in its parts to about 1 us each. That it meets the medians to 0.3 us is luck: for the parts that it priced the traces give -8.3, and for the whole -6.4, 2.8 us less than forecast. The fall behind the last turning is probably in both kernels most of the time and so drops out of the medians; the one at chunk 1 belongs to the change.

Rivals 1 (narrow records at 0.15, or waits before the later turnings) and 4 (wide multiplies of `wo1` at half clock) did not occur: the clock is 1.00 throughout `wo1`, the records took 0.106, and no later turning inside it waits. Rival 3 occurred in part: the clock rose 2.5 us earlier in both profiles of the changed kernel, though in e1, e7 and e8 it rose as late as before.

## What to carry to other kernels

In this kernel narrow work with waits between engines cost least inside a long row of wide multiplies on TensorE, for two reasons at once: its waits were covered, and it ran at the full clock. Putting it there moves the bound to whatever lay beside it before, so such an edit has to be priced together with the reorderings that only then begin to count (0.15 us alone, 3.4 us together). Steps added to an evacuation were nearly free (0.5 us over seven hand-overs) until the slack at the hand-over was used, and then cost their full length each time, although their engine was idle for a quarter of the stretch.

## What the runs showed of the hardware

- The granted clock does not follow TensorE's momentary work. It fell near 486.4 in e4, 0.7 us after the engine was back at wide multiplies. In e3 it fell at 477 among narrow multiplies (busy for 1.40 of the 2 us before) and stayed at 0.50 through 15 us of which the engine was busy 12.65. It rose 3.4 to 6.2 us after the gather's first multiply at half clock (3.5 in the changed kernel, 6.1 before the change, 6.2 in e7).
- Waits of 2.5 to 3.5 us between rows of wide multiplies were followed by a fall in 13 of 18 cases (4 of 7 at chunk 1, 9 of 11 at the last turning), each costing about 1.6 us, eight multiplies or so at 0.43 instead of 0.23 us, and once 2.9 us (e11, 14 multiplies). The same wait of 2.91 us behind the same last stage was followed by a fall in e9's profile and by none in that of the kernel before.
- Multiplies that compute nothing, put into such waits, were worth 4 to 5 us in a kernel of 851 us (e5 against e10; 4.2 by the traces, and 0.979 and 0.985 of before in separate comparisons). In e4 the first of them did not hold the clock, in e5 they did.
- The same kernel's early part varies by several microseconds: in e1's profile the clock between 30 and 60 us is 0.83, in the changed kernel's 0.96, and the first turning comes 6.9 us later.
